# Experts 1 and 2 run as two units of rows, the first during the routing of the last token tile

## The reference

```python
def hierarchical_moe(h, router_group_w, router_group_b, router_expert_w, router_expert_b, w_gate, w_up, w_down):
    g_idx = jnp.argmax(g_logits, axis=-1)
    ...
    top_w, top_i = lax.top_k(jax.nn.softmax(e_logits, axis=-1), TOP_K_EXPERTS)
    expert_id = g_idx[:, None] * EXPERTS_PER_GROUP + top_i
    combine = jnp.sum(jax.nn.one_hot(expert_id, N_EXPERTS, dtype=jnp.float32) * (g_w * top_w)[..., None], axis=1)
    gate = jnp.einsum('nd,edf->nef', h, w_gate)
    up = jnp.einsum('nd,edf->nef', h, w_up)
    act = jax.nn.silu(gate) * up * combine[..., None].astype(h.dtype)
    return jnp.einsum('nef,efd->nd', act, w_down)
```

## Time and profile before

| | |
|---|---|
| median of three runs | 777.72 us |
| profiled execution | 773.9 us, of which the span shown is 771.7 us |
| PE busy | 716.1 us, 93% of the span |
| expert stage (first gate product to last down product) | 480.3 to 745.4 us |
| DMA in the whole span | 172.96 MB, mean 224 GB/s |
| mean granted PE clock | 0.974 of full |

### The profile page before, as it was taken

How to read it: one execution, slowest core, us unless ns; L and a number is a source line. 1 busy time by engine, 2 the same in 40 slices (tenths; PEclk the granted TensorE clock), 3 DMA queues, 4 the chain that set the end, 5 groups by cost and what they waited for, 6 DMA issues and landing times.

```text
span 771.7 us, 12386 instructions
## 1 busy us (share of the span) xinstructions
PE 716.1 (93%) x4681; PEld 383.0 (50%) x4681; DVE 345.0 (45%) x743; ACT 218.4 (28%) x561; POOL 126.5 (16%) x175
## 2 busy tenths in 40 slices
PE   6988999999999989989999994999999999999987
PEld 2446456444554445445555642465456454454532
DVE  5521103595213464746846655383334343223246
ACT  1121111122312646566587621011111110011113
POOL 0111100120001623333332412100000000000050
PEclk9999999999999989999999996999999999999999
DMA  8156880677757610000000195997999999999992
GB/s 328 47 149 186 229 302 30 230 239 226 223 198 202 254 41 1 1 3 1 21 8 1 35 360 157 379 342 258 400 399 403 409 405 402 408 389 410 411 366 111
DMA packets 99565, 172.96 MB, mean 224 GB/s; under 512 B 21330, under 2 KB 38706, under 8 KB 99474
## 3 DMA queue, kind: packets, MB, share of 16 engines
q1 hardware_dynamic: 80290, 142.40, 51.7%
q10 hardware_dynamic: 15952, 19.59, 7.4%
q0 software_dynamic: 3264, 10.17, 3.7%
HBM read 152.95 MB, written 21.28 MB: 226 GB/s over the span
## 4 chain that ended last, share of the span: by engine, by line
PE 73%; issue 10%; DMA 5%; ACT 4%; DVE 4%; POOL 2%; ACTq 1%; SPq 0%; DVEq 0%; POOLq 0%
PE bank L2508 18%; PE bank L2956 13%; PE bank L1910 6%; PE bank L2938 6%; PE bank L2499 5%; PE bank L2542 4%; PE bank L1848 3%; PE bank L1827 3%; PE bank L1706 2%; PE bank L1861 2%; DMA x<-x_prompt 1%; PE bank L2632 1%; PE bank L2627 1%; PE bank L2960 1%; PE bank L1829 1%
## 5 line engine op out<-in xcount | busy, mean ns | idle before, releaser
L2956 PE MATMUL bank<-reg 128*128 128x512 f32 (+1 forms) x352 | 149.5, 571 | 1.2 <-DVE reg L2893 0.9
L2508 PE MATMUL bank<-reg,qreg 128*32 128x128 f32 (+2 forms) x848 | 130.0, 388 | 0.8 <-issue 0.8
L2508 PEld LDWEIGHTS bank<-reg,qreg 128*32 128x32 f32 (+2 forms) x848 | 66.7, 139 | 59.2 <-issue 47.8
L2956 PEld LDWEIGHTS bank<-reg 128*128 128x128 f32 x352 | 65.6, 195 | 60.6 <-issue 56.4
L1215 POOL TENSOR_SCALAR reg<-reg,st,gates 128x128 f32<-128x128 f32 (+3 forms) x64 | 41.2, 652 | 183.9 <-DVE st L1502 183.8
L2938 PE MATMUL bank<-cf,reg 128*128 128x128 f32 (+1 forms) x384 | 61.3, 278 | 10.8 <-DVE rt L1671 3.8
L1910 PE MATMUL bank<-reg 128*128 128x512 f32 x128 | 62.8, 614 | 0.4 <-DVE x L1614 0.3
L2938 PEld LDWEIGHTS bank<-cf,reg 128*128 128x128 f32 (+1 forms) x384 | 41.6, 141 | 30.9 <-issue 25.1
L2798 ACT ACTIVATE work<-bank 128x128 f32<-128x128 f32 (+5 forms) x107 | 40.8, 411 | 41.0 <-PE bank L2938 39.6
L2157 POOL DMA_INDIRECT work<-h_rows,ids x15 | 13.9, 929 | 195.8 <-PE bank L2555 113.6
L2893 DVE COPY work<-bank 128x128 f32<-128x128 f32 (+4 forms) x55 | 22.8, 429 | 50.3 <-PE bank L2938 50.3
(11 more groups left out here) (350 smaller groups left out, 941.7 us busy)
## 6 DMA issues: line engine op xcount, KB each, us to landing
reg<-w_gate SPq DMA_DIRECT2D x12, 2048.0 KB, 19.3
reg<-w_up SPq DMA_DIRECT2D x12, 2048.0 KB, 21.0
reg<-w_down SPq DMA_DIRECT2D x12, 2048.0 KB, 20.7
reg<-w_in ACTq DMA_DIRECT2D x16, 512.0 KB, 6.0
expert_rows<-vreg SPq DMA_DIRECT2D x11, 512.0 KB, 6.3
reg<-cache_sb_k SPq DMA_DIRECT2D x16, 256.0 KB, 4.3
reg<-cache_sb_v SPq DMA_DIRECT2D x16, 256.0 KB, 4.4
qreg<-w_up SPq DMA_DIRECT2D x2, 2048.0 KB, 17.2
```

The lines of the kernel that those rows point to most:

```text
L2508: ins = T.matmul(bank[which][rows, at_:at_ + w], rowsT[b][:, k, r0:r0 + n], w_[:, k, h * w:(h + 1) * w], start=(k == 0), stop=(k == KD - 1))
L2956: ins = nc.tensor.matmul(at("m", ("proj", n))[:, 0:w], hT[:, k, i * P:(i + 1) * P], win[:, pos % 2, k, 0:w], start=(k == 0), stop=(k == KD ...
```

## The change

`FIXED = (1, 2, 0)`: experts 1, 2 and 0 come first, in this order, the others as before by their counts. `SIZES` has 1344 places instead of 1440: three experts of 128 rows instead of six, six of 96 instead of three, and five of 64 and two of 32 as before.

Experts 1 and 2, with 96 places each, run together as two units. Unit 0 holds up to 64 rows of each from the tiles known before the last (the sample tile and tiles 0 to 2); unit 1 holds up to 32 rows of each from the last tile. Unit 0's rows are gathered in a step of its own (`early_gather`), right after tile 2 has been ranked, while the output projection of tile 3 runs; their transposes (`early_rows`) stand before the last four products of that projection. The 32 steps of gate and up products of unit 0 (`fill`, two products of 64 columns each) are spread in portions of 2, 2, 1, 6, 2, 10 and 9 among the routing steps of tile 3. Unit 1's rows are not gathered: `last_rows` multiplies tile 3's rows h2, still on the core, with a one-hot matrix `last_pick`, which gives them transposed at once. Unit 1's gate and up products then follow as the first step of the expert loop, unit 0's down products after them, and unit 1's down products after the gate and up of the next expert.

The routing of tile 2 is moved earlier among the products of tile 3, and its h2 rows are stored by ACT's queue instead of SP's. The ranks of experts 1 and 2 are counted with two more columns, with some short DVE instructions more in `slots` and `count`. Ring loads 6 and 7 get waits of their own: number 6 waits for the last product of tile 3's projection, number 7 for `last_rows` and the h2 stores. Loads 8 to 13 wait for the second of the two units, where they waited for expert 0 or expert 1 (`max(j, 1) + 1`). Three more blocks of 128 rows for the loop of extra rows and one block of `h_rows` are cleared in memory early in the program.

With the inputs of the reference, experts 1 and 2 get 48 and 58 rows from the tiles before the last, and 17 and 16 from the last; no expert has more rows than places, in either version.

```diff
-SIZES = (P, 96, 64, 32, P, 64, 96, 96, P, 32, P, P, 64, P, 64, 64)
-BY_RANK = list(SIZES[:2]) + sorted(SIZES[2:], reverse=True)
+FIXED = (1, 2, 0)
+EARLY_ROWS, LAST_ROWS = 64, 32
+SPLIT = slice(FIXED[0], FIXED[1] + 1)
+SIZES = (96, 96, P, 64, 96, 64, P, 32, 96, 64, P, 32, 96, 96, 64, 64)
+BY_RANK = list(SIZES[:3]) + sorted(SIZES[3:], reverse=True)
+UNITS = (2 * EARLY_ROWS, 2 * LAST_ROWS) + SIZES[2:]
...
-EXTRA = 10
+EXTRA = 13
...
-    return j if j < 2 else 2 + sum(n > SIZES[j] for n in SIZES[2:]) + sum(n == SIZES[j] for n in SIZES[2:j])
+    return j if j < 3 else 3 + sum(n > SIZES[j] for n in SIZES[3:]) + sum(n == SIZES[j] for n in SIZES[3:j])
...
+def unit_blocks(u):
+    if u < 2:
+        n = (EARLY_ROWS, LAST_ROWS)[u]
+        return [(n * j, n, j, first_row(j) + EARLY_ROWS * u) for j in range(2)]
+    return [(r0, n, u, first_row(u) + r0) for r0, n in BLOCKS[SIZES[u]]]
...
-        if i == QT - 1:
-            use("x", ("ids0",), "dve")
-            step("ids0")
-            sg.mark("ids0", 0)
+    def route_slots(i):
...
+    def early_ids():
+        use("x", ("ids0",), "dve")
+        step("early_ids")
+        step("early_gather")
+        sg.mark("e_x0", "early", 16)
+    def early_rows():
+        use("o", ("rows0",), "act")
+        use("x", ("rows0",), "dve")
+        step("early_rows")
+    filled = [0]
+    def fill(n):
+        for m in range(filled[0], filled[0] + n):
+            step("fill", m // (2 * KD), m // KD % 2, m % KD)
+        filled[0] += n
...
-    def rest_of_rows(i):
-        ffn_squares(i)
-        ffn_scale(i)
-        ffn_rows(i)
...
-    rest_of_rows(QT - 2)
+    ffn_squares(QT - 2)
+    ffn_scale(QT - 2)
...
-    for n in range(16):
+    product(QT - 1, 0)
+    route_parts(QT - 2)
+    product(QT - 1, 1)
+    ffn_rows(QT - 2)
+    store_rows(QT - 2)
+    route_group(QT - 2)
+    route_choice(QT - 2)
+    for n in range(2, 5):
...
-        if n == 7:
-            step("chunk", 5)
-        if n % 4 == 3:
-            add_product(QT - 1, n // 4)
-        if n == 4:
-            mix_scales(QT - 1)
-        if n == 5:
-            route_parts(QT - 2)
-        if n == 8:
-            route_group(QT - 2)
-            route_choice(QT - 2)
-        if n == 12:
-            rank(QT - 2)
-    for half in range(2):
-        transpose_ffn(QT - 1, half)
-    rest_of_rows(QT - 1)
+    mix_scales(QT - 1)
+    rank(QT - 2)
+    product(QT - 1, 5)
+    early_ids()
+    add_product(QT - 1, 0)
+    route_slots(QT - 2)
+    for n in range(6, 8):
+        product(QT - 1, n)
+    step("chunk", 5)
+    add_product(QT - 1, 1)
+    for n in range(8, 12):
+        product(QT - 1, n)
+    add_product(QT - 1, 2)
+    early_rows()
+    for n in range(12, 16):
+        product(QT - 1, n)
+    transpose_ffn(QT - 1, 0)
+    step("chunk", 6)
+    add_product(QT - 1, 3)
+    fill(2)
+    transpose_ffn(QT - 1, 1)
+    ffn_squares(QT - 1)
+    ffn_scale(QT - 1)
+    fill(2)
...
+    ffn_rows(QT - 1)
...
+    fill(1)
...
+    fill(6)
...
+    route_slots(QT - 1)
+    fill(2)
+    step("last_rows")
+    for name in ("e_rowsT_full", "e_rows_a", "e_rows_v"):
+        sg.mark(name, "last")
+    step("chunk", 7)
+    use("x", ("count",), "dve")
+    step("count")
+    sg.mark("turns", 0)
+    fill(10)
+    use("x", ("order",), "dve")
+    step("order")
...
+    fill(9)
...
+        sp.dma_start(h2_dram[(QT - 1) * P:QT * P, :], vsb[:, 0:2, :].rearrange("p a b -> p (a b)")).then_inc(sg["y_zero"], 16)
...
-            if i == QT - 1:
+            if i in (QT - 2, QT - 1):
...
-        elif kind == "ids0":
+        elif kind == "early_ids":
...
+        elif kind == "early_rows":
+            pe.wait_ge(sg["e_x0"], 16)
+            for half, ring in enumerate("ox"):
+                acquire(pe, ring, ("rows0",))
+                for k in range(4):
+                    kk = 4 * half + k
+                    ins = T.transpose(at(ring, ("rows0",))[:, k * P:(k + 1) * P], rows_in[0][:, kk * P:(kk + 1) * P], ident)
+                ins.then_inc(sg[ring + "_full"], 1)
+        elif kind == "fill":
+            which, e, k = key
+            rows_at, w = EARLY_ROWS * e, FF * EARLY_ROWS // P
+            if k == 0:
+                wait_chunk(pe, ("gate", "up")[which], e)
...
+            for rows, h in column_groups(EARLY_ROWS):
+                ins = T.matmul(bank[which][rows, w * e:w * e + w], rowsT[0][:, k, rows_at:rows_at + EARLY_ROWS],
+                               chunk(("gate", "up")[which], e)[:, k, h * w:(h + 1) * w], start=(k == 0), stop=(k == KD - 1))
+            if e == 1 and k == KD - 1:
+                ins.then_inc(sg[("e_gate", "e_up")[which]], 1)
+        elif kind == "last_rows":
+            sg.wait(pe, "rows0", QT - 1)
+            sg.wait(pe, "h2", QT - 1)
+            sg.wait(pe, "o_act", ("rows0",))
...
+            for half, to in enumerate((bank[3], bank[6])):
+                for k in range(4):
+                    kk = 4 * half + k
+                    ins = T.matmul(to[:, k * UNITS[1]:(k + 1) * UNITS[1]], h2[:, kk * P:(kk + 1) * P], last_pick[:, :],
+                                   start=True, stop=True)
+                ins.then_inc(sg["e_rowsT_full"], 1)
...
                 sp.wait_ge(sg["st_v"], sg.total["st_v"])
+            elif n == 5:
+                sg.wait(sp, "m_full", ("wout", QT - 1, 1))
+            elif n == 6:
+                sg.wait(sp, "m_full", ("wout", QT - 1, 3))
             else:
-                sg.wait(sp, "m_full", ("wout", QT - 1, 1))
-            load_chunk(sp, n, CHUNKS[n][1])
+                sp.wait_ge(sg["e_rowsT_full"], 2)
+                sp.wait_ge(sg["st_h2"], sg.total["st_h2"])
+            load_chunk(sp, n, FIXED[CHUNKS[n][1]])
         elif kind == "experts":
-            sg.wait(sp, "t_full", ("logit", QT - 1))
-            sp.wait_ge(sg["st_h2"], sg.total["st_h2"])
-            sp.wait_ge(sg["e_x0"], 16)
             sg.wait(sp, "x_dve", ("order",))
-            expert_reg = [0, 1]
+            expert_reg = list(FIXED)
...
-            for n in range(6, len(CHUNKS)):
+            for n in range(RING, len(CHUNKS)):
                 if CHUNKS[n][0] == "gate":
                     next_expert(CHUNKS[n][1])
-                if n >= RING:
-                    before, j = CHUNKS[n - RING]
-                    sp.wait_ge(sg["e_" + before], j + 1)
+                before, j = CHUNKS[n - RING]
+                sp.wait_ge(sg["e_" + before], max(j, 1) + 1)
                 load_chunk(sp, n, expert_reg[CHUNKS[n][1]])
...
     def expert_gps(pool, kind, key):
-        if kind == "ids0":
-            sg.wait(pool, "ids0", 0)
-            pool.wait_ge(sg["st_h2"], sg.total["st_h2"])
+        if kind == "early_gather":
+            sg.wait(pool, "x_dve", ("ids0",))
+            sg.wait(pool, "st_h2", QT - 2)
             sg.wait(pool, "pv", turned[-1])
-            sg.wait(pool, "t_full", ("parts", QT - 1))
             nc.gpsimd.indirect_dma_start(rows_in[0], None, h2_dram,
...
             sg.wait(pool, "x_dve", ("idx",))
-            for j in range(1, NE):
-                if j >= 2:
-                    pool.wait_ge(sg["e_rowsT_full"], 2 * (j - 2) + 2)
+            for j in range(2, NE):
+                if j == 2:
+                    pool.wait_ge(sg["st_h2"], sg.total["st_h2"])
+                    sg.wait(pool, "x_full", ("rows0",))
+                else:
+                    pool.wait_ge(sg["e_rowsT_full"], 2 * (j - 2))
                 nc.gpsimd.indirect_dma_start(rows_in[j % 2][0:SIZES[j]], None, h2_dram,
...
-                b, w_ = j % 2, chunk(("gate", "up")[which], j)
-                for r0, n in BLOCKS[SIZES[j]]:
-                    w, at_ = FF * n // P, FF * r0 // P
+                b = j % 2
+                for r0, n, e, _ in unit_blocks(j):
+                    w, at_, w_ = FF * n // P, FF * r0 // P, chunk(("gate", "up")[which], e)
+                    wait_chunk(pe, ("gate", "up")[which], e)
...
-            sort_experts()
-            rows_of(0)
-            for j in range(NE):
-                pe.wait_ge(sg["e_rows_a"], j + 1)
-                pe.wait_ge(sg["e_rows_v"], j + 1)
-                wait_chunk(pe, "gate", j)
-                if j > 0:
-                    pe.wait_ge(sg["e_gated"], 3 * j)
+            sort_ids()
+            for j in range(1, NE):
+                pe.wait_ge(sg["e_rows_a"], j)
+                pe.wait_ge(sg["e_rows_v"], j)
+                pe.wait_ge(sg["e_gated"], 3 * j)
...
-                if j == 0:
-                    sort_ids()
-                if j > 0:
-                    pe.wait_ge(sg["e_act"], j)
-                    transpose_acts((j - 1) % 2, 4 * SIZES[j - 1] // P, sg["e_actT_full"])
-                wait_chunk(pe, "up", j)
+                pe.wait_ge(sg["e_act"], j)
+                transpose_acts((j - 1) % 2, 4 * UNITS[j - 1] // P, sg["e_actT_full"])
...
-                if j > 0:
-                    finish_down(j - 1)
+                finish_down(j - 1)
```

(10 more changed lines are left out.)

186 lines of the change are left out of this document (121 added, 65 removed).

## The result

The changed kernel takes 782.59 us (median of 11 runs, 778.72 to 786.85), the kernel before in the same comparison 774.77 (11 runs, 772.49 to 779.01). The ratio is 1.0079, with a 95% interval from 1.0051 to 1.0108; it is taken over all fast runs and is not the quotient of the two medians, which would be 1.0101. Run a second time on another chip the kernel gave 1.0102 (1.0076 to 1.0128). It is 6 to 8 us slower. 774.5 was forecast, with 780.5 as the upper end.

What follows compares the result with a forecast made beforehand. Weight loads were taken to end the expert stage, with PE nearly level. The last matrix 2.2 us sooner and 1.0 in the tail made -3.2 us, from 777.7 to a median of 774.5; range 767.5 to 780.5.

Steps and rivals of the forecast that it cites:

- the wait for the early gather: PE before the early-row transposes (L2033): rows there at 464.5 after store and gather of 7.0 us each, wait 3.7 us.
- The start: Everything up to the issue of ring load 3: taken as unchanged, load 3 at 441.0 us.
- the 57 small DVE instructions: Expert stage, after gate and up of the third unit: costed at nothing, because PE waits for loads there.
- From there to T: From PE ready for the early rows (19.8 us behind load 3) to the last projection's end (28.0).
- T: End of the last tile's projection: 463.9 us before, forecast 469, bounds 465.5 to 474.
- late gather and half clock: Slower rival, before L2033: rows at 469.0, T 473.5, half clock 1.7 us twice, S 535, time 782.5; chance 0.13.
- S: Moment from which ring loads run without a pause: 532.85 us before, forecast 527, then with load 12.
- T to S: From the last projection's end through routing and first units to loads 12 and 13 issued together: 58 us.
- S to the last matrix: Expert stage under uninterrupted loads: 209.7 us plus 3.6 for more bytes at 404 GB/s, last matrix at 740.3.
- The tail: Down 13, its store, gathers: 1.5 us less product, store in six pieces instead of one, 1.0 us gained.
- the 13 us that PE saves: Expert stage, three experts of 128 rows made 96: 13 us of PE, hidden beside the loads, worth nothing until loads come sooner.

Runs made afterwards that it cites:

- e10: The changed kernel with 1440 places instead of 1344 (turns 4, 8 and 13 with 128 rows): 780.24 us, 1.0039 of the kernel before.
- e11: The changed kernel with early-row transposes behind the projection, unit 1's down product sooner, early-row picks later, and 1440 places: 772.53 us, 0.9936 of the kernel before.
- e2: The changed kernel with the places of turns 9 and 13 exchanged, the last stored expert having 64 instead of 96: 785.18 us, 1.0097 of the kernel before.

## Why the prediction was wrong

The forecast for the profiled execution was a span of 768.5 us (771.7 - 3.2); it was 780.8. The step that failed is the wait for the early gather: the prediction gave it 3.7 us and nothing for the clock behind it. The 12.3 us, step by step from the table of the first section:

**The start, +3.7.** I took everything ahead of the last tile as unchanged. Part of that was a step of mine: "the 57 small DVE instructions after gate and up of the third unit (PE waits for loads there)" were costed, but the ones that the change adds to the ranks of each earlier tile were not. PE waited for them 0.56 us longer at 332 and 0.60 at 389, in both profiles of the changed kernel: 1.2 us. The rest of the 3.7 is one drop of the clock near 236 us, which cost 3.0 us (what came ahead of it was 0.4 sooner). It is in the first profile of the changed kernel and not in that of the kernel before; here the windows of 225 to 245 us, before and after:

```profile
225.00:245.00 20.00, 18.99 (x128) 10.67 (x129) 3.96 (x17) 2.34 (x8) 0.89 (x2) 1.00 0.76 219
```

```profile
225.00:245.00 20.00, 18.98 (x109) 10.48 (x99) 2.90 (x14) 1.93 (x7) 0.00 (x0) 0.83 0.75 223
```

This drop has nothing to do with the change: the other three profiles without it have it too, at 0.83 or 0.91. Of fourteen profiles only that of the kernel before and that of e10 are without it. A second drop may be the change's: in the windows of 325 to 345 us the clock stood at 1.00 in three of the four profiles without the change, and at 0.83 or 0.91 in all ten with it. It is no part of the 3.7, because the kernel before is the fourth (0.91, as in the first profile after), but it can be part of the later load 3 in the mean. That the longer wait brings the drop is not shown: with the wait cut to 2.09 us the clock still fell.

**From there to T, +4.2: the failed step.** "[...] the rows are there at 464.5." and "PE waits 3.7 us, then 1.1 for eight transposes and 3.6 for the last products: T = 469." PE was ready at 19.7 as forecast (19.8). The store, from its issue at 454.01 to the gather's at 462.60, took 8.6 us and the gather 7.4 instead of 7.0 each, so the rows came 1.9 late (the gather waited for nothing else: its row numbers were there at 459.3, and the store's packets moved from 457 to 462). And behind the wait of 5.68 us the transposes cost 0.9 and the products 1.5 more at half clock. I had each of these effects in the rival (late gather and half clock), with a chance of 0.13, and had taken the forecast's wait of 3.7 us as harmless, though the earlier trace rows shows half clock behind a wait of 4.5 us. By the rows, 3.7 lay nearer to that than to nothing. Taking L2033 out of the way gave some 6 us back. That the rival's time, 782.5, is the measured 782.6 is luck: counted from load 3 it had T, with its half clock, at 34.2 and S at 94.0 (measured 32.2 and 88.9), and nothing for the start, nor for a longer tail.

**T to S, -1.3.** 58 forecast, 56.7 and 58.3 measured: right. So was its form, PE's short wait before the first unit (2.0 us for 2.5) and loads 12 and 13 together.

**S to the last matrix, +1.5.** From S to the last down product 214.7 and 215.3 us, forecast 213.3 (209.7 + 3.6). The rate between 680 and 720 us was 404 GB/s. Right.

**The tail, +4.2.** "Down 13 has 96 rows now, 1.5 us less, but its store goes out in six pieces instead of one; I count 1.0 of gain." The six pieces take 3.17 us of ACT's queue, so from the end of the product to the first gather 11.2 us pass instead of 9.0 (734.5 to 745.69; 728.5 to 737.47 before): a loss of 0.7 with the shorter product, which the kernel with fewer places alone confirms (0.8). Half clock added 1.7 in down 13 and 1.7 in the final products, and from the first gather to the first final product 9.2 us passed instead of 10.0; together the 3.2 by which the tail grew (forecast was 1.0 less, hence 4.2). In the second profile of the same kernel the clock did not fall there and the tail is 29.4. The sign of the term was wrong, which is 1.7 of the 4.2; the rest is where the clock fell, and differs by the execution. PE idles more because it has fewer rows to work on: 198.9 us busy of 217 from 533 us on, before 213.1. With 1440 places the tail was 28 us.

These give 3.7 + 4.2 - 1.3 + 1.5 + 4.2 = 12.3.

What held: loads set the end of the expert stage, and the 13 us that PE saves are worth nothing. What I had only half seen is that PE was level with the loads ("nearly level, and the DMA engines have the last word"); where S comes sooner in the kernel before, PE's saving is needed, as the sooner down product shows (nothing alone, 0.5% with fewer places). In the changed kernel it is not needed even then (e11). The likely reason, not shown, is that gate and up of unit 0, some 15 us by the prediction, have already left the expert stage there. The change put these savings of PE into a kernel where the loads came no sooner: it moves S forward from 91.9 to 88.9 us behind load 3, but S is one load earlier in the ring there, and a load is worth 5.2 us (2.1 MB at 404 GB/s). The last down product starts 303.7 us behind load 3, before 301.6. The Trainium skill (DMA: Bandwidth & Descriptors, Issuing engines are not separate DMA queues) says that transfers of all issuing engines interleave on the same 16 engines. The gathers beside the last two ring loads agree, 42.4% against 59.3% of them, and this is what I should have carried over to the tail.

## What to carry to other kernels

Where two engines end level, test an edit for each together: alone, either reads as nothing. A step that waits for a transfer belongs behind the work that doesn't need it, even if it is short, for PE paid for the wait twice here, the second time in clock (5.7 us and 2.4). And before a thread in the tail is made faster, look for what its transfers will share the DMA engines with: here gathers 6.5 us sooner held the last weight matrix back by 4.

## What the runs showed of the hardware that was not expected

- Gathers of 512 KB each, issued every 1.24 us, took 42.4% of the DMA engines beside the last two 2 MB ring loads (2.26 MB against 3.15 MB in 13 us, e2). That the last ring load had been issued 11 us ahead of the first gather did not keep it ahead: its product started 9.1 us behind the one before instead of 4.9.
- Waits of PE of some 2 us in an otherwise busy stretch were followed by a lower clock: between 331 and 343 us the granted clock fell to half, 1.2 GHz, in ten of ten profiles with waits of 2.1 to 2.5 us there, and in one of four with waits of 1.95. Near 390 us it fell in all fourteen, behind waits of 1.85 us in one of them, so the length of a wait alone does not tell.
- Executions of kernels that differ little up to there are several us apart before the expert stage alone (load 3 from 441.2 to 448.6 us with the change), in part by where the clock drops: one drop near 236 us cost 3.0. A single pair of profiles can't tell 3 us there; the step that it is put down to needs several.
